# Constant products put into TensorE's waits across a two-block language model kernel

## What is computed

```python
h = x + hybrid_mixer(rms_norm(x), ...)       # projection, convolution, gated delta rule, SSD, output product
h = h + expert_choice_ffn(rms_norm(h), ...)  # 16 experts, each takes its 64 best tokens (top_k over tokens)
x = rms_norm(h)
for i in range(2):                           # second block, 528 rows with 16 meta tokens ahead
    h = layer_norm(ALPHA * h + mix)          # projection, windowed attention, convolution, w_out
    f = swiglu(h) if i == 0 else moe_swiglu(h)   # layer 1: 8 experts, top 2 for each token
    h = layer_norm(ALPHA * h + f)
```

```python
u_new = u_c - w_c @ S
o = qd_c @ S + qk_c @ u_new
S = S * exp(gl_c) + kd_c.T @ u_new
```

## Time and profile before

| | |
|---|---|
| three runs | 3065.92, 3068.12 and 3073.71 us, median 3068.12 |
| profiled execution | 3069.07 us, its span 3067.3 us |
| PE busy | 2845.1 us (93%), 18486 matmul records |
| DVE busy | 1298.7 us (42%) |
| ACT busy | 635.7 us (21%) |
| mean granted clock of PE | 0.961 |

### The profile page before, as it was taken

The page is one execution under the profiler, slowest core; times in us unless marked ns, Lnnn a source line. Parts: engine busy times, 40 slices in busy tenths (PEclk is TensorE's granted clock), DMA queues, the critical chain, the costliest instruction groups (busy, mean ns, idle before and its releaser), DMA issues. The chain is left out here.

```text
span 3067.3 us, 44164 instructions
## 1 busy us (share of the span) xinstructions
PE 2845.1 (93%) x18486; PEld 1858.6 (61%) x18486; DVE 1298.7 (42%) x2338; ACT 635.7 (21%) x1505; POOL 278.6 (9%) x233
## 2 busy tenths in 40 slices
PE   8998899999969998998999999899898899999896
PEld 7764787654433337866678888788684444444343
DVE  6875666564131237931443335588314211111014
ACT  3553233322011113234011110022420000000001
POOL 0001322350000000011400000000122100000000
PEclk9998899999979998999999999999998899999998
DMA  3213000107089952212032212012021642667916
GB/s 121 83 69 61 4 17 17 56 14 287 21 334 428 428 229 93 83 49 114 10 132 92 93 48 76 30 74 110 21 98 61 234 180 79 243 243 324 380 69 277
DMA packets 81800, 412.71 MB, mean 135 GB/s; under 512 B 10547, under 2 KB 21683, under 8 KB 65892
## 3 DMA queue, kind: packets, MB, share of 16 engines
q1 hardware_dynamic: 71508, 385.99, 32.2%
q10 hardware_dynamic: 6816, 12.33, 1.3%
q0 software_dynamic: 3312, 12.06, 1.0%
HBM read 381.59 MB, written 28.76 MB: 134 GB/s over the span
## 5 line engine op out<-in xcount | busy, mean ns | idle before, releaser
L4185 PE MATMUL pgu<-gu,xg 128*64 128x320 f32 (+1 forms) x2560 | 394.9, 464 | 7.1 <-POOLq L4113 7.1
L4185 PEld LDWEIGHTS pgu<-gu,xg 128*64 128x64 f32 x2560 | 182.6, 138 | 204.0 <-issue 130.8
L4192 PE MATMUL py<-down,hm_t 128*64 128x512 f32 x880 | 200.0, 602 | 11.1 <-POOLq L4113 11.1
L3112 DVE SCALAR_TENSOR_TENSOR conv<-vg,cols,conv 128x528 f32<-128x528 f32 x240 | 164.3, 760 | 0.0
L4254 DVE TENSOR_TENSOR hm<-sg,pgu 128x384 f32<-128x384 f32 (+1 forms) x40 | 20.8, 521 | 314.0 <-PE pgu L4185 207.3
L4192 PEld LDWEIGHTS py<-down,hm_t 128*64 128x64 f32 x880 | 62.0, 139 | 122.7 <-issue 104.7
L698 DVE SCALAR_TENSOR_TENSOR mixed<-padded,taps,mixed 128x512 f32<-128x512 f32 x144 | 102.6, 749 | 41.5 <-ACT mixed L519 39.4
L4137 ACT ACT_TABLE_LOAD x19 | 24.4, 1283 | 459.8 <-PE pgu L4185 279.1
L3612 DVE TENSOR_TENSOR gb<-gb,pp 128x264 f32<-128x264 f32 x66 | 28.2, 429 | 174.7 <-PE pp L3524 174.7
L426 PE MATMUL proj<-feat,w 128*128 128x512 f32 x192 | 84.4, 592 | 0.0
L2857 PE MATMUL pp<-feat,w 128*128 128x264 f32 (+1 forms) x320 | 82.1, 407 | 0.0
(11 more groups left out here) (642 smaller groups left out, 5359.1 us busy)
## 6 DMA issues: line engine op xcount, KB each, us to landing
gu<-in_moe_gu SPq DMA_DIRECT2D x16, 3072.0 KB, 9.9
gu<-in_moe_gu SPq DMA_DIRECT2D x16, 2560.0 KB, 15.5
ring<-in_w_gate SPq DMA_DIRECT2D x16, 2048.0 KB, 11.9
ring<-in_w_up SPq DMA_DIRECT2D x16, 2048.0 KB, 15.2
ring<-in_w_down SPq DMA_DIRECT2D x16, 2048.0 KB, 17.3
w<-in_w_in SPq DMA_DIRECT2D x13, 2048.0 KB, 7.6
down<-in_moe_down SPq DMA_DIRECT2D x8, 3072.0 KB, 18.7
down<-in_moe_down SPq DMA_DIRECT2D x8, 2560.0 KB, 20.7
```

What stands on the lines that cost most here:

```text
L3112: dve.scalar_tensor_tensor(out=out, in0=glu[:, c, j:j + NTOK], scalar=tap(c, j), in1=out, op0=ALU.mult, op1=ALU.add).then_inc(own, 1)
L4185: last = pe.matmul(pgu[half(h), part, 0:n], xg[:, k, :], w[:, k, h, :], start=k == 0, stop=k == DK - 1)
L4192: last = pe.matmul(py[half(h), :], hm_t[:, c, :], down[:, c, h * BANK:(h + 1) * BANK], start=c == 0, stop=c == XC - 1)
```

## The change

A method `keep_clock(pe, bank, n)` is added. It multiplies the constants, identity times the first 256 columns of `core.cst`, `n` times into a bank that nobody reads at that point. It waits for nothing itself. It is called at these places of PE's list, nowhere else:

- in `gated_delta`, by `pace`, in the periods in which `r` is None, that is the first two: 14 ahead of the first period, and 2 behind each step of `s` and of `i`: 5 steps in the first period, 15 in the second;
- in `ssd_and_output`, 6 ahead of the last tile's transposes;
- in `expert_choice_route`, 3 behind the router, 3 behind the transpose of the logits, then 4 behind each of nine waits, for the copy of the affinities and for each of the 8 rounds;
- at the end of `expert_choice_ffn`, 14, 12, 6 and 3 ahead of the turns of tiles 1 to 4, and 3 behind the last;
- at the end of both `mix_layer`, 4, 10 and 3, and of `dense_ffn`, 10 and 3;
- in `route_top_two`, 3, 7, 10 and 6.

That makes 213 products. Nothing is removed, and no other engine's list changes.

```diff
+    def keep_clock(self, pe, bank, n):
+        for _ in range(n):
+            pe.matmul(bank[:, 0:2 * P], self.cst[:, ID0:ID0 + P], self.cst[:, 0:2 * P], start=True, stop=True)
...
+                def pace(r, n=2):
+                    if r is None:
+                        core.keep_clock(pe, pr[:, 0, 0, :], n)
+
                 def period(s, i, r, za, zb):
+                    if i is None:
+                        pace(r, 14)
                     if za is not None:
                         gate_unit(za)
                     if s is not None:
                         keys_keys(s)
+                        pace(r)
                     if i is not None:
                         level_x(i, 1)
+                        pace(r)
...
+                pe.wait_ge(out_read, TILES + 1)
+                core.keep_clock(pe, out[0], 6)
                 turn_rows(TILES - 1)
...
                 last.then_inc(p_sem, 1)
+                core.keep_clock(pe, px[:, 0, :], 3)
                 pe.wait_ge(lt_out, TILES)
                 pe.transpose(pl[:, 0:P], lt[:, :], ident).then_inc(p_sem, 1)
+                core.keep_clock(pe, px[:, 0, :], 3)
...
+                for r in range(CAP // 8 + 1):
+                    pe.wait_ge(v_sem, AFF + 1 + 2 * r)
+                    core.keep_clock(pe, px[:, 0, :], 4)
                 pe.wait_ge(v_sem, CHOSEN)
...
-                for n in range(len(rows)):
+                for n, fill in enumerate((0, 14, 12, 6, 3)):
+                    core.keep_clock(pe, py[:, 0, :], fill)
                     norm.turn(pe, n, banks)
+                core.keep_clock(pe, py[:, 0, :], 3)
...
+                core.keep_clock(pe, bank_y(PAIRS2 - 1), 4)
                 norm.turn(pe, first + TILES - 2, banks)
+                core.keep_clock(pe, bank_y(PAIRS2 - 1), 10)
                 norm.turn(pe, first + TILES - 1, banks)
+                core.keep_clock(pe, bank_y(PAIRS2 - 1), 3)
...
+                core.keep_clock(pe, bank_y(3), 10)
                 norm.turn(pe, TILES, banks)
+                core.keep_clock(pe, bank_y(3), 3)
...
+                core.keep_clock(pe, px, 3)
                 pe.wait_ge(lt_out, TILES)
                 pe.transpose(pl[:, 0:P], lt[:, :], ident).then_inc(made, 1)
+                core.keep_clock(pe, px, 7)
                 pe.wait_ge(own, SELECTED)
...
                 last.then_inc(counted, 1)
+                core.keep_clock(pe, px, 10)
                 pe.wait_ge(weights.first_found, 1)
...
                 last.then_inc(weights.first_turned, 1)
+                core.keep_clock(pe, pr, 6)
```

## The result

| | before | changed |
|---|---|---|
| median (lowest to highest, runs) | 3069.92 us (3063.3 to 3076.0, 9) | 3078.45 us (3068.58 to 3079.93, 9) |
| profiled execution, its span | 3069.07 us, 3067.3 | 3077.15 us, 3075.4 |
| mean granted clock of PE | 0.961 | 0.980 |
| PE busy | 2845.1 us | 2901.2 us |

A forecast was written before the change was run, and what follows sets the result against it. The prediction took PE's time to bound the kernel, with only work at 1.2 GHz open to shortening. Terms -9 + 4 + 4.6 + 8 gave 7.6 us gained, a median of 3060.5 us; range for 8 in 10: 3053 to 3071.

The forecast's parts named there:

- MoE's route: Last MoE's route: 8 us gained, 6.9 of it in the gather at full clock, with the scatter not holding the block.
- A constant product: Price of each added product on PE: 0.43 us at 2.4 GHz, 0.86 at 1.2 GHz.
- Delta, 9 us lost: gated_delta: 5.4 us lost in its first period, 4.3 in its second, 0.5 gained in its third; between 6 and 11.
- First period: Start of gated_delta: the 14 products take 8.3 us, faster groups give back 4.1; with the pairs, 5.4 us lost.
- the second period: gated_delta's second period: 14 pairs cost 12.1 us, waits hide 4, the higher clock returns 3.8; 4.3 us lost.
- Expert choice, 4 gained: Expert choice's route: faster router, slots' turn and first gather outweigh products that overrun the rounds; end about 4 us earlier.
- The reading by which the router would stay at 1.2 GHz: Expert choice: if transposes don't count as PE activity, the router stays slow and the gain there is 2.1 us.
- Block ends, 4.6 gained: Behind the first MoE, mix_layer of layer 0 and dense_ffn: next blocks start at higher clock; 4.6 us gained, between 1 and 6.
- the first rival: Last MoE's route: the gather loses its clock, the block starts 2 us earlier, not 8; 3066.5 us, chance 0.2.
- pairs cost little: gated_delta: the clock outlasts DVE's first level in both periods, so the delta loses 4; 3055.5 us, chance 0.15.
- What is already late takes the gains: Behind block ends, sums or weights hold the next starts, and expert choice keeps 2 of 4; 3068 us, chance 0.11.
- The rival of the slower side: All added products: constants, mostly zeros, don't lift the clock, so each costs 0.86 us; 3163 us, chance 0.04.

The follow-up runs named there:

- e1: The changed kernel, with SP waiting for all eight scatters before the first unit's remaining weight loads in expert_ffn: 3065.99 us, ratio to before 0.9983.
- e2: The changed kernel with 20 constant products instead of 6 behind the gather of route_top_two: 3069.04 us, ratio to before 0.9982.
- e3: The kernel before, with only SP's added wait for the scatters and no constant products: 3070.85 us, ratio to before 0.9994.
- e5: The kernel before, with only route_top_two's constant products (3, 7, 10 and 6): 3072.2 us, ratio to before 1.0003.
- e10: The changed kernel with SP's wait for the scatters and, in the delta, only the 14 products ahead of the first period: 3061.23 us, ratio to before 0.9977.
- e4: The changed kernel without the delta's constant products and without SP's wait for the scatters: 3069.8 us, ratio to before 0.9988.
- e9: The changed kernel with SP's wait for the scatters and no constant products in the delta: 3059.43 us, ratio to before 0.9968.
- e11: The changed kernel with SP's wait for the scatters and, in the delta, only the pairs behind the steps: 3057.96 us, ratio to before 0.996.

## Why the prediction was wrong

The step that failed is in the MoE's route: "POOL's scatter, whose places come 2.5 us earlier, ends at 2388.96 - 2.5 = 2386.5 and does not hold it." The end of POOL's issue was taken for the end of the scatter. The issue ended at 2387.21 (2386.24 and 0.97), 0.7 us later than said, since the places came 1.8 us earlier and not 2.5; but the data landed at 2406.02. The block's end does not wait for the data; its readers in the next block do. Two questions were left out. The first is whether the data can keep pace with an earlier issue: they could not, the DMA engines being full. The second is what the earlier opening sets off: SP's weights, ahead of the scatter's last rows. e1 and e2 show by two different changes that the time comes back when SP's loads start later, and e3 that nothing was lost there before. PE's wait was 14.88 us in the profile, of which e1 leaves 6.92 and e2 0.32; timed, either takes off 13 us, give or take 5. What stays open is why the weights stretched the scatter's end here and not in e5, which opens its block early too and was not slower than before. The profile's sum is then -4.8 + 14.9 - 2.0 (gained in the expert units behind) = 8.1 us, the difference of the spans.

The other steps, each against its own number:

- **A constant product**: 0.43 us at full clock. Right ahead of the gather: 20 records, 4.56 us, so 0.44 each with the end taken off. A pair amid other shapes held back the next product by 0.86 to 1.06 us, where 0.86 was forecast.
- **Delta, 9 us lost**: 9.06, but by parts that were off, so that the match is luck. First period 6.2, not 5.4: the 14 took 9.1, at the far end of the 7.3 to 9 that I gave (whose lower end was wrong too: 14 at 0.43 are 6.0 us, and 4 to 6 us at 1.2 GHz add 2 to 3).

```profile
291.67 9.10 PE L110 MATMUL pr<-cst 128*128 128x256 f32 x28 [7.28 <-PEq L357]
300.60 1.05 PE L947 MATMUL pz<-chan 128*128 128x128 f32 x8
...
315.89 1.08 PE L975 MATMUL pxy<-tc,am 32*32 32x32 f32 x64 [4.76 <-DVE tc L1279]
316.90 2.08 PE L110 MATMUL pr<-cst 128*128 128x256 f32 x4
...
347.14 0.75 PE L975 MATMUL pxy<-tc,am 32*32 32x32 f32 x64 [2.17 <-DVE tc L1279]
```

  The fall of the clock in the wait for the first level came (4.76 us of wait, then 2.08 for a pair), but low clock lasted from 314.4 to 321.2, some 5 us behind that wait (it ended at 315.89) and not 3. With the longer pairs the second period lost 7.3, not 4.3. The rest gave back 4.5, not 0.5, and it is not shown that this was the fills' doing (last section).
- **Expert choice, 4 gained**: 2.97. The router took 1.94 and the first gather of rows 3.84 us; the turn of the slots began at 882.89, 1.4 us behind DVE's last row of slots, which ended at 881.45 (forecast 1.1).

```profile
860.34 1.94 PE L2095 MATMUL pr<-feat 128*16 128x128 f32 x64 [1.80 <-PEq L1509]
...
867.15 15.81 PE L110 MATMUL px<-cst 128*128 128x256 f32 x72 [0.84 <-DVE work L2166]
882.89 0.42 PE L2111 MATMUL ps<-cst,slot 16*128 16x16 f32 x4
884.02 3.84 PE L2081 MATMUL px<-feat,chan 128*128 128x128 f32 x32 [0.71 <-DVE feat L2179]
```

  The reading by which the router would stay at 1.2 GHz behind its transposes, and the sum be 2.1, is refuted by the first of these rows; whether the six products or the transposes held the clock is not told apart. But 1.7 us were given back at once: "the experts behind it were PE's throughout" was wrong, since they wait for rows loaded by DMA, 2.22 us at 908.15, and the clock fell for some 3 us around 900 and again around 910. Before, it fell there once, from 892 to 895, and a wait of 2.18 us at 902.42 did not bring it down.
- **Block ends, 4.6 gained**: from 1143 to 2365 the difference goes from 7.40 to 1.05, 6.35 gained. Blocks began 0.3 us early, 0.2 late and 0.9 late as forecast; the first products of `dense_ffn` took 7.36 us for 9.72. Most of the surplus lies in layer 1's attention, where nothing was changed: before, the clock was at 0.50 from 2166 to 2170 us behind a wait of 2.83, and in the changed kernel that wait was 1.68 and the clock stayed up. One loss had no term: behind a wait of 2.98 us inside `dense_ffn` the same 22 records took 6.67 us before, 7.98 in the changed kernel and 4.99 in e1, whose list of PE is the same there. Timelines of PE, changed and e1:

```profile
1946.77 7.98 PE L3726 MATMUL pd<-sums_t,hm 128*128 128x256 f32 x22 [2.98 <-DVE hid L3799]
```

```profile
1945.17 4.99 PE L3726 MATMUL pd<-sums_t,hm 128*128 128x256 f32 x22 [2.98 <-DVE hid L3799]
```

- **MoE's route, 8 gained**: 5.82 up to the first expert product. The gather held its clock (7.25 us, forecast 7.0), so the first rival fell. What is missing lies behind it. DVE's copy of `px` began 2.7 us after the last product had ended (2385.80), which it did not do before; and POOL's queue held the first expert product 4.05 us in place of 3.15. DVE's timelines, changed and before:

```profile
2388.45 0.69 DVE L3921 COPY xg<-px 128x512 f32<-128x512 f32 x1 [5.43 <-remote]
```

```profile
2394.17 0.69 DVE L3880 COPY xg<-px 128x512 f32<-128x512 f32 x1 [9.38 <-PE px L3963]
```

  The gap is the same with 6, 20 or 3 products behind the gather (5.4 to 5.7 us behind DVE's previous instruction). Its reason stays open.
- **The rivals**: "pairs cost little" fell as it was put, since the clock did not outlast DVE's first level and the second period lost 7.3 us. "What is already late takes the gains" was the right kind of case but named sums and weights, not the scatter. The rival of the slower side, clock not lifted by constants, fell: the 14 brought it up.

## What to carry to other kernels

When a stage is made shorter, list what it issued and nobody has yet waited for, and what the next stage will issue the moment it opens: the slack of slow work may be what lets a transfer land. An end of issue in a row is not the end of the data; read the DMA share of the windows between the two. Filling a wait is free only if the products are fewer than the wait is long; ahead of work that is ready they cost their full length, less what the higher clock gives back behind them (in e10 the 14 took 9.2 us and made the delta's first stretch 5.4 us longer).

## What the runs showed of the hardware

- From the last issue of the scatter to its landing it took 10.12 us by itself (chain of e1, below), at most 7.4 before, and beside the weights 19.76 us in the changed kernel and 23.25 in e4, but 9.92 in e5. ACT's two loads of 128 KB behind it took 12.95 us beside weights in the changed kernel and 13.88 in e5.

```profile
2383.24 10.12 DMA moe_rows<-hid,place
```

- 64-column products at 1.2 GHz ran 13.92 us without lifting the clock, and at 2.4 GHz ran 7.25 us without losing it.
- The clock at the start of the delta is partly chance: e9 has no fills there, and its window reads 0.81 where before has 0.50.

```profile
288.00:318.00 30.00, 17.44 (x507) 15.34 (x508) 13.83 (x28) 8.16 (x17) 14.36 (x12) 0.81 0.15 48
```

- From 340 to 572 us, where nothing was changed and the clock was full nearly throughout, PE paused inside its groups of 32x32 products for no cause that the profile shows. Waits of PE there, before, changed and e11 (us, times, longest):

```profile
PE pxy L969 <- issue: 6.3, 11, 1.1
```

```profile
PE pxy L975 <- issue: 4.7, 5, 1.2
```

```profile
PE pxy L975 <- issue: 2.0, 4, 0.6
```

  These pauses are part of the difference in the table's "rest" (241.8, 237.3 and 232.1 us). Why they differ stays open, and so does how much of the delta's loss goes by them.
